# A hybrid decoder layer on one core: the first MLP layer by seven half-size products per pair of units, and the MLP in eight blocks of four tiles

## The reference

```python
x = x + gt1 * mix
h2 = rmsnorm(x, norm2_g) * (1.0 + sc2) + sh2
x = x + gt2 * (jnp.square(jax.nn.relu(h2 @ w_ff1)) @ w_ff2)
...
y = rmsnorm(x, final_g)          # D_MODEL = 1024, D_FF = 4096
```

## Time and profile before

| | us |
|---|---|
| median of 3 runs (lowest, highest) | 1261.55 (1257.51, 1267.34) |
| the profiled execution | 1263.77 |
| its span, first to last instruction | 1262.0 |
| TensorE busy in it | 1195.5 (7549 matmuls) |
| VectorE, ScalarE, GpSimd busy | 439.0, 401.8, 431.5 |

### The profile page before, as it was taken

One profiled execution on the slowest core, in us unless ns is written; L12 is line 12 of the kernel. 1 busy time (PEld: TensorE's weight loads), 2 busy tenths in 40 slices (PEclk: granted clock), 3 DMA queues, 4 the chain that ended last, 5 costly groups with the idle time before them and its releaser, 6 DMA issues.

```text
span 1262.0 us, 19541 instructions
## 1 busy us (share of the span) xinstructions
PE 1195.5 (95%) x7549; PEld 1143.7 (91%) x7549; DVE 439.0 (35%) x812; ACT 401.8 (32%) x675; POOL 431.5 (34%) x322
## 2 busy tenths in 40 slices
PE   4899999789988999999999999999999999999997
PEld 2698888679876899899999999999999999999996
DVE  4651445367785434631111122111121111211125
ACT  4642445335334334543111233111333101332121
POOL 0431111100543348664322344221444212444441
PEclk9999989879987999999999999999999999999998
DMA  9704424535531721111111111111110111111103
GB/s 313 271 32 133 118 79 153 171 109 182 171 106 63 252 101 68 67 35 50 51 50 36 48 50 50 51 33 50 50 50 33 50 50 50 41 43 50 33 1 135
DMA packets 56301, 109.73 MB, mean 87 GB/s; under 512 B 6418, under 2 KB 28854, under 8 KB 55862
## 3 DMA queue, kind: packets, MB, share of 16 engines
q1 hardware_dynamic: 46038, 84.88, 19.9%
q10 hardware_dynamic: 10208, 24.12, 6.1%
HBM read 96.81 MB, written 12.18 MB: 86 GB/s over the span
## 4 chain that ended last, share of the span: by engine, by line
PE 78%; DVE 9%; DMA 6%; ACT 3%; SPq 2%; issue 1%; POOL 0%; ACTq 0%; DVEq 0%; POOLq 0%
PE D L1707 24%; PE D L1709 23%; PE D L1708 23%; DMA RAWW<-in_WADA 2%; PE X L1678 1%; PE X L1734 1%; PE X L1735 1%; PE X L1736 1%; DMA X0T<-in_x 1%; DMA out_C_p<-CN 1%; DMA NM<-nm_d 1%; DVE FU L1271 1%; PE X L1692 1%; DVE X L1285 1%; DVE FU L1475 1%
## 5 line engine op out<-in xcount | busy, mean ns | idle before, releaser
L1707 PE MATMUL D<-H_hi,W_hi 128*128 128x344 f32 x1144 | 376.9, 329 | 2.0 <-POOL H_lo L825 1.3
L1708 PE MATMUL D<-H_lo,W_hi 128*128 128x344 f32 x1144 | 369.4, 323 | 0.0
L1709 PE MATMUL D<-H_hi,W_lo 128*128 128x344 f32 x1144 | 369.0, 323 | 0.0
L820 POOL TENSOR_TENSOR W_lo<-RAWW,W_hi 128x1024 fp32r<-128x1024 f32 x84 | 201.7, 2401 | 410.9 <-ACT W_hi L962 409.7
L1707 PE MATMUL D<-Y_hi,W_hi 128*128 128x344 f32 x936 | 300.9, 321 | 3.1 <-issue 2.9
L1708 PE MATMUL D<-Y_lo,W_hi 128*128 128x344 f32 x936 | 299.6, 320 | 0.0
L1709 PE MATMUL D<-Y_hi,W_lo 128*128 128x344 f32 x936 | 299.6, 320 | 0.0
L1707 PEld LDWEIGHTS D<-H_hi,W_hi 128*128 128x128 f32 x1144 | 219.1, 192 | 12.5 <-issue 8.4
L1708 PEld LDWEIGHTS D<-H_lo,W_hi 128*128 128x128 f32 x1144 | 218.8, 191 | 0.7 <-issue 0.2
L1709 PEld LDWEIGHTS D<-H_hi,W_lo 128*128 128x128 f32 x1144 | 218.5, 191 | 0.0
L825 POOL TENSOR_TENSOR Y_lo<-FU,Y_hi 128x344 f32 (+3 forms) x120 | 113.6, 949 | 230.2 <-ACT Y_hi L967 229.9
(11 more groups left out here) (280 smaller groups left out, 946.0 us busy)
## 6 DMA issues: line engine op xcount, KB each, us to landing
RAWW<-in_W SPq DMA_DIRECT2D x76, 512.0 KB, 3.2
RAWW<-in_WADA ACTq DMA_DIRECT2D x28, 512.0 KB, 4.3
RAWW<-in_WADA SPq DMA_DIRECT2D x20, 512.0 KB, 7.5
RAWW<-in_W ACTq DMA_DIRECT2D x18, 512.0 KB, 3.3
X0T<-in_x SPq DMA_DIRECT2D x3, 1376.0 KB, 9.4
X<-in_x SPq DMA_DIRECT2D x8, 516.0 KB, 6.2
out_y<-OUTN SPq DMA_DIRECT2D x24, 172.0 KB
NM<-nm_d SPq DMA_DIRECT2D x8, 256.0 KB, 4.6
```

The source lines that it names most:

```text
L820: nc.gpsimd.tensor_tensor(lo_v, RAWW[:, raw, :] if src is None else src[:], hi_v.bitcast(F32), ALU.subtract).then_inc(w_lo_ready, 1)
L1707: T.matmul(out, w_h, hi[:, kt, a:b], start=(kt == 0), stop=False)
L1708: T.matmul(out, w_h, lo[:, kt, a:b], start=False, stop=False)
L1709: one = T.matmul(out, w_l, hi[:, kt, a:b], start=False, stop=(kt == KT - 1))
```

## The change

For 14 of the 16 pairs of first-layer units, chunks 1 and 2 are computed by Strassen's method in Winograd's form. Take a pair's weights as A11, A12 (first unit, first and last four tiles of the input) and A21, A22 (second unit), and the input as B11, B21 (chunk 1, first and last four tiles) and B12, B22 (chunk 2). Instead of eight half-size products there are seven: A11 by B11, A12 by B21, S2 by T2, S1 by T1, S3 by T3, A22 by T4, S4 by B22, with S1 = A21+A22, S2 = S1-A11, S3 = A11-A21, S4 = A12-S2 (VectorE, once per pair) and T1 to T4 likewise of the input (once in all; each is split in hi and lo too). The seven land in five PSUM banks X0 to X4; VectorE adds them up (`summed`, `joined`) through three SBUF tiles `KEPT`. Chunk 0 is computed as before (`direct`). The first four units stay as they were.

The MLP becomes `FF_PARTS` = 8 blocks of four hidden tiles: two pairs of the first layer, then 24 second-layer products of four tiles each (12 matmuls) instead of 24 of eight. The weights' hi and lo now lie in a ring of six half-unit places (`place`), which ScalarE (`ring`) and VectorE (`low`) write; GpSimd no longer makes weights' lo parts in the MLP. A load for the second layer has the four tiles of two units (two pieces of 2 KB per partition). `B1` and `B2` hold the second norm's output of chunks 1 and 2, which no longer passes through `FU`. The loop now runs over whole blocks: blocks 0, 1 and 7 are written out, five are one loop. The last block takes units 4 to 7 chunk by chunk, and half of chunk 1's final pieces come after the last inverse.

```diff
--- before.py
+++ after.py
...
 FF_BLOCKS = 4
+FF_T = 4
+FF_PARTS = KT // FF_T * FF_BLOCKS
...
+        HALF_AT = {"A11": 0, "A12": 1, "S2": 2, "S1": 3, "S3": 4, "A21": 5, "A22": 6, "S4": 7}
...
+        SEVEN = {"A11": ("X0", 0), "A12": ("X1", 0), "S2": ("X2", 0), "S1": ("X3", 0), "S3": ("X4", 0), "A22": ("X0", 1), "S4": ("X1", 1)}
...
+        def place(l, n=1):
+            k = (l + 4) % 6
+            assert k % 2 + n <= 2
+            return tuple(t[k // 2][:, (k % 2) * HALF:(k % 2 + n) * HALF] for t in (RING_HI, RING_LO))
...
+        PIECES = [(0, 0), (0, 1), (1, 2), (1, 0), (1, 1), (0, 2)]
...
+        def second_steps(last):
+            out = [(0, k % 2, k // 2) for k in range(2 * NCH)] + [(1, k // NCH, k % NCH) for k in range(2 * NCH)]
+            if last:
+                return out + [(2 + k % 4 // 2, k % 2, k // 4) for k in range(4 * NCH)]
+            return out + [(f, k // NCH, k % NCH) for f in (2, 3) for k in range(2 * NCH)]
...
+            def ring(b, i, name):
+                prev = (b[0], b[1] - 1)
+                if name == "F":
+                    act.wait_ge(raw_in[raw_tile(FF_T + i)], raw_landed(b, FF_T + i))
+                elif name[0] == "A":
+                    t = 2 * i + (name != "A1")
+                    act.wait_ge(raw_in[raw_tile(t)], raw_landed(b, t))
+                else:
+                    act.wait_ge(sums_ready, per_pair(b, i, 4, {"S2": 2, "S1": 2, "S4": 3, "S3": 4}[name]))
+                if name == "F":
+                    if is_first(b):
+                        if i in (0, 2):
+                            act.wait_ge(d_full[NCH - 1], D_FIRST + 2 + i)
+                    elif i == 0:
+                        seven_there(act, b, 1, "S2")
+                        seven_there(act, b, 1, "S1")
+                    elif i == 1:
+                        seven_there(act, b, 1, "S3")
+                        act.wait_ge(d_full[1], direct_at(b, 1))
+                    elif i == 2:
+                        seven_there(act, b, 1, "A22")
+                        seven_there(act, b, 1, "S4")
+                    if i == 3:
+                        act.wait_ge(d_full[NCH - 1], second_at(b, NCH - 1, 2))
+                elif name == "A22":
+                    seven_there(act, b, i, "A11")
+                elif name == "S4":
+                    seven_there(act, b, i, "A12")
+                elif i == 0:
+                    n = {"A1": 4, "S2": 5, "S1": 6, "S3": 7, "A21": 8}[name]
+                    act.wait_ge(d_full[NCH - 1], second_at(prev, NCH - 1, n))
+                elif name == "A1":
+                    seven_there(act, b, 0, "S2")
+                    seven_there(act, b, 0, "S1")
+                elif name == "S2":
+                    seven_there(act, b, 0, "S3")
+                elif name == "S1":
+                    act.wait_ge(d_full[1], direct_at(b, 0))
+                elif name == "S3":
+                    seven_there(act, b, 0, "A22")
+                elif name == "A21":
+                    seven_there(act, b, 0, "S4")
+                nc.scalar.activation(ring_half(i, name)[0], ring_source(i, name), ACT.Copy).then_inc(ring_hi, 1)
...
+            def keep_first(b, i):
+                seven_there(act, b, i, "A11")
+                nc.scalar.activation(KEPT[0][:], seven_bank("A11"), ACT.Copy).then_inc(first_kept, 1)
+            def pair(b, i):
+                ring(b, i, "A21")
+                if i:
+                    hi_piece(b, 0, 5)
+                relu_piece(b, i, 0)
+                hi_piece(b, i, 0)
+                keep_first(b, i)
+                ring(b, i, "A22")
+                ring(b, i, "S4")
+                hi_piece(b, i, 1)
+                if i == 0:
+                    ring(b, 1, "A1")
+                    ring(b, 1, "S2")
+                else:
+                    ring(b, 0, "F")
+                hi_piece(b, i, 2)
+                relu_piece(b, i, 1)
+                if i == 0:
+                    ring(b, 1, "S1")
+                else:
+                    ring(b, 1, "F")
+                hi_piece(b, i, 3)
+                if i == 0:
+                    ring(b, 1, "S3")
+                hi_piece(b, i, 4)
...
+            def t_sum(n):
+                b11, b21, b12, b22 = (t[:, k:k + FF_T, :] for t in (B1, B2) for k in (0, FF_T))
+                if n == 0:
+                    dve.wait_ge(lo_ready, P_FF)
+                    one = V.tensor_tensor(b22, b22, b12, ALU.subtract)
+                elif n == 1:
+                    one = V.tensor_tensor(b12, b12, b11, ALU.subtract)
+                elif n == 2:
+                    one = V.tensor_tensor(b11, b22, b11, ALU.add)
+                else:
+                    one = V.tensor_tensor(b21, b21, b11, ALU.subtract)
+                tell(one, t_summed, n + 1)
+            def low(b, i, name):
+                dve.wait_ge(ring_hi, ring_at(b, i, name))
+                hi_v, lo_v = ring_half(i, name)
+                V.tensor_tensor(lo_v, ring_source(i, name), hi_v.bitcast(F32), ALU.subtract).then_inc(ring_lo, 1)
+                if name[0] == "S":
+                    dve.wait_ge(ring_lo, ring_at(b, i, name))
...
+            def sums_12(b, i):
+                for t in (2 * i, 2 * i + 1):
+                    dve.wait_ge(raw_in[raw_tile(t)], raw_landed(b, t))
+                tell(V.tensor_tensor(SB[:], raw_half(2 * i + 1, 0), raw_half(2 * i + 1, 1), ALU.add), sums_ready, per_pair(b, i, 4, 1))
+                tell(V.tensor_tensor(SA[:], SB[:], raw_half(2 * i, 0), ALU.subtract), sums_ready, per_pair(b, i, 4, 2))
+            def sum_4(b, i):
+                tell(V.tensor_tensor(SA[:], raw_half(2 * i, 1), SA[:], ALU.subtract), sums_ready, per_pair(b, i, 4, 3))
+            def sum_3(b, i):
+                tell(V.tensor_tensor(SB[:], raw_half(2 * i, 0), raw_half(2 * i + 1, 0), ALU.subtract), sums_ready, per_pair(b, i, 4, 4))
+            def slot_of(b, i, q):
+                dve.wait_ge(lo_ready, piece_at(b, i, q) - (FUS - 1))
+                return FU[:, piece_tile(i, q)[3], 0:CH]
...
+            def joined(b, i, q, name, k):
+                fu = slot_of(b, i, q)
+                seven_there(dve, b, i, name)
+                tell(V.tensor_tensor(fu, seven_bank(name), KEPT[k][:], ALU.add), seven_free[SEVEN[name][0]], seven_at(b, i, name))
+                V.scalar_tensor_tensor(out=fu, in0=fu, scalar=0.0, in1=fu, op0=ALU.max, op1=ALU.mult).then_inc(full_ready, 1)
+            def summed(b, i, name, src, dst):
+                seven_there(dve, b, i, name)
+                one = V.tensor_tensor(KEPT[dst][:], seven_bank(name), KEPT[src][:], ALU.add)
+                if name == "S1":
+                    link(one)
+                else:
+                    tell(one, seven_free[SEVEN[name][0]], seven_at(b, i, name))
...
+            def pair(b, i):
+                if i:
+                    joined(b, 0, 5, "S4", 2)
+                low(b, i, "A21")
+                squared(b, i, 0)
+                low(b, i, "A22")
+                dve.wait_ge(first_kept, per_pair(b, i, 1, 1))
+                joined(b, i, 1, "A12", 0)
+                low(b, i, "S4")
+                summed(b, i, "S2", 0, 1)
...
+                    sums_12(b, 1)
+                summed(b, i, "S1", 1, 2)
+                if i == 0:
+                    low(b, 1, "A1")
+                else:
+                    low(b, 0, "F")
+                summed(b, i, "S3", 1, 1)
+                joined(b, i, 2, "S1", 1)
+                if i == 0:
+                    low(b, 1, "S2")
+                    sum_4(b, 1)
+                squared(b, i, 3)
+                if i == 0:
+                    low(b, 1, "S1")
+                    sum_3(b, 1)
+                else:
+                    low(b, 1, "F")
+                joined(b, i, 4, "A22", 1)
+                if i == 0:
+                    low(b, 1, "S3")
+            def residual(b, o, f, h, c):
...
+            def next_part(b, o):
+                after = (b[0], b[1] + 1)
+                if o == 13:
+                    low(after, 0, "A1")
+                elif o == 14:
...
+                for o, (f, h, c) in enumerate(second_steps(False)):
+                    residual(b, o, f, h, c)
+                    if o == 1:
+                        low(b, 2, "F")
+                    elif o == 7:
+                        low(b, 3, "F")
...
-                    final(0, range(6, KT))
+                elif QUAD + 5 <= o <= QUAD + 7:
+                    k = 2 * (o - QUAD - 5)
+                    final(0, range(k, k + 2))
+                elif o == QUAD + 8:
                     inverse_diagonal(1)
...
+                elif o == QUAD + 10:
+                    final(1, (0,))
+                elif o == QUAD + 11:
+                    final(1, range(1, 4))
             inverse_diagonal(NCH - 1)
+            final(1, range(4, KT))
             final(NCH - 1, range(POOL_FIN, KT))
 
 
@@ -1882,13 +2243,69 @@
                     pe.wait_ge(d_free[bank], g * 2 + (first - SKEW + v))
```

(43 more changed lines are left out.)

499 lines of the change are left out of this document (304 added, 195 removed).

## The result

The changed kernel takes 1229.85 us (median of 4 runs, 1229.13 to 1230.67), the kernel before 1261.8 us beside it (4 runs, 1257.51 to 1267.34). The profiled execution took 1229.13 us, its span is 1227.2.

The account below looks back on a forecast made before the run. TensorE was taken as the bound, busy 95% of the span. Terms -26.4 + 2.1 + 0.5 + 0.5 = -23.3 us on 1263.8 gave 1240.5, or 1238.3 from the runs' median, stated as 1239; range 1233 to 1253.

Parts of the forecast that it names:

- the base and the lower end of the range: Whole kernel: profiled 1263.8 us as base, runs' median 2.2 lower; range reaching down to 1233 by the runs' own spread.
- The removed matmuls: MLP on TensorE: 168 fewer matmuls at 0.1574 us each save 26.4 us.
- Rival 4: TensorE in the MLP: starts of groups set the pace, so 330 products for 192 eat the saving; no chance given.
- The opening piece: Each second-layer start: the hidden piece read first comes 0.3 us late, 2.1 us over seven blocks, bounds 0 and 8.4.
- Rival 1: VectorE's strict order delays last pieces around 1.2 us per block start or pair: 8.4 instead of 2.1, about 1245; chance 0.15.
- These edits I cost at nothing: Weight copies and lo parts in the MLP's ring of places: weights arrive in time, cost 0.
- The step into the MLP: Entry to the MLP: VectorE's input sums and lo parts delay piece 9, costing 0.5 us, bounds 0 and 2.
- The tail: Behind the last inverse: four more VectorE pieces and queued stores cost 0.5 us, bounds 0 and 1.5.
- Rival 2: MLP loop: body too long to be kept, four jumps back stall TensorE, 12 to 20 us, 1251 to 1259; chance 0.12.
- Rival 3: Second-layer starts: lateness of about 3.5 us per block drops TensorE's clock, 34 us for seven blocks, 1272; chance 0.06.

Follow-up runs that it names:

- e1: The kernel before, unchanged, run again: 844.4 us from the first output-projection product to the end of the span, instead of 841.5.
- e4: The kernel before with only its small buffers moved to the SBUF places the change gives them: ratio 0.9988 to the kernel before.
- e10: The kernel before, unchanged, once more: output projection starts at 415.23 us.
- e11: The kernel before, unchanged, a second copy: output projection starts at 411.69 us.
- e3: The changed kernel with each pair's A11 product done twice, putting 168 matmuls back: MLP 709.82 us, from 683.38.
- e5: The changed kernel with VectorE's lo part of F1 behind the join of piece 4 in each block's second pair: MLP 1.04 us shorter.
- e7: The changed kernel with two unused VectorE additions between relu and square of the piece opening the second layer: MLP 689.64 us, 6.26 added.
- e6: The changed kernel with VectorE's lo parts of F2 and F3 later, in the first block only: MLP 0.52 us shorter.
- e8: The changed kernel with five unused VectorE additions ahead of the opening piece's square: MLP 29.28 us longer, ratio 1.0013 to the kernel before.

## Why the prediction was off, step by step

**The step that failed: the base and the lower end of the range.** The prediction says that the range "reaches down by the runs' own spread: 1233". I had taken the part ahead of the MLP as a constant, read from one execution, with 2.2 us between it and the median of three runs as its only uncertainty. It isn't one: the start of the output projection stands anywhere between 411.7 and 423.8 us in five profiles of the old form and between 410.2 and 422.5 in nine of the new. The profile that I worked from was a late one (420.45), and the first four runs of the changed kernel were luck: 1229.13 to 1230.67, at the low end of its sixteen, which go to 1244.5. The same kernel in two other sessions took 1233.9 and 1234.3 us, at the lower edge of the range but in it. The 29 runs of the kernel before beside e1 to e4 go from 1253.5 to 1271.7 us, down to 7.6 below their median; that much below 1238.3 would have been 1230.7, at the edge of what was measured. The terms of the change were not the fault: I had them at 23.3 us together, and the stages give 24.56 less 0.6 and 0.3 (below), 23.7. What the sum also lacked is a term for the part ahead of the MLP, which I had at nothing; by the run times of the next paragraph it is about 4 us.

How much of the 32 us is real? The stages give 24.56 - 0.6 = 24 us. The three comparisons of the unchanged pair gave 32, 27 and 31 us less on the whole (1229.85 to 1261.8, 1233.9 to 1261.06, 1234.34 to 1265.24). The mean of all sixteen runs of the changed kernel is 1234.3 us, that of the 92 of the kernel before in the same sessions (e1, e10 and e11 among them) 1262.4: 28.1 us less, to within some 2.6 by the scatter of the runs. e3 says the same: by its stages it should be 2.5 us longer than the kernel before, and its median is 0.3 shorter. The stages agree with both only if the part ahead of the MLP gave something too. Its end, the first landmark, stands at 540.3 us in the mean of the five old forms and at 537.1 in that of the nine new ones, 3.2 us earlier in spite of the longer wait there; 2.1 of it is there at the start of the output projection (417.8 and 415.6), the rest is the late load of e1 and e11. With a spread of 4 us in each group this difference of means alone could be chance. Another reading of the profiles goes the same way: in the first 40 us the nine new forms made 134 to 146 matmuls, mean 142, the five old ones 126 to 136, mean 133; at 100 us the distance is still 10, at 6.6 matmuls per us 1.5 us. The places of the small buffers are not its cause (e4 has 126). What is, and whether the distance holds in more copies, stays open. So 24 us are shown to come from the change, some 4 more are likely by the run times but not explained, and the rest of the first pair's 32 is chance. Why the clock falls there in one execution and not in the next stays open as well.

**The removed matmuls, -26.4.** Right: 26.44 in e3. Rival 4 (group starts eat the saving) is out by the same number and by the block's period, 86.83 us in e5.

**The opening piece, +2.1 (0.3 x 7; bounds 0 to 8.4).** Right in mechanism, half in size: 1.04 us by e5, 0.16 in each turn of the loop and some 0.1 in the blocks before and behind it. The chain went as forecast up to VectorE's hold, but Y_lo, started 0.81 us before the lo part's end, finished 0.78 behind it where I had 0.95. That difference of 0.17 is about what the forecast of 0.3 was too high. Rival 1 (1.2 us per block) asked for another 1 us of lateness in VectorE's list; no row of the changed kernel shows it. e7, where the piece is 1.0 us later, shows what it would have cost: 6.3 us more, as much as the 8.4 - 2.1 = 6.3 that I had between it and the forecast.

The row which the prediction lacked, GpSimd as the loser, is there now: 1.59 us instead of 0.93 when VectorE holds, and VectorE 3.89 instead of 1.22 when GpSimd does. The Trainium skill, page "SBUF — State Buffer", section "Who interferes with whom", says that the first to issue blocks the other fully. The trace agrees with the order in both directions. The whole instruction is not held back, though: Y_lo would then have ended at 641.24 + 0.93 = 642.17, and it ended at 642.02. VectorE's lo part beside T_lo likewise ended 1.08 us behind T_lo and not 1.22. So some 0.15 us of the second one runs beside the first, whichever it is.

**The cost that I put at nothing and was not: the weights of the first block, +0.5.** "These edits I cost at nothing" covered the lo parts of F2 and F3 beside GpSimd's lo parts of T. I had seen that overlap for the squares in the step into the MLP, and had GpSimd's T_lo in the same paragraph, but did not put the two lists side by side for VectorE's new work. By e6 it is 0.52 us.

**The step into the MLP, +0.5.** Measured 0.6 (1.00 against 0.39 us of wait, and the same in all nine new-form profiles). **The tail, +0.5.** From the last square to the end of the span there are 11.2 to 12.7 us in the five old-form profiles and 11.7 to 12.9 in the nine new ones, mean 11.8 and 12.1: 0.3, within the scatter. All stall terms together: 3.1 forecast, 1.9 in the MLP and 0.6 to 0.9 outside it measured. With every term right, the sum would still have been 1263.8 - 26.4 + 2.6 = 1240.0 on the profiled execution.

**Rival 2, the loop body.** Out: no idle time without a releaser in the MLP, turns of the loop as long as the written-out block once the opening stall is gone (86.83 us, e5), and 42 instruction packets instead of 34 for the whole run.

**Rival 3, the clock.** It didn't happen, but e8 shows that its mechanism and its point were right: with a stall of 3.25 us per block nothing is left of the gain, where the prediction had "about 3.5 us per block". Only its price per dip was high, 1.6 us and in five of seven cases, where I had 2 in each.

## What to carry to other kernels

Before summing up terms of a few tenths of a microsecond, measure how far the unchanged part repeats: one profile gives the size of a stage but not where it stands, and the range of a forecast on the whole is at least that of the old kernel's own runs. Measure an edit by the time between two landmarks that enclose only what it touches; here it repeats to 0.01 us while the total moves by 10. A part that the edit doesn't touch needs as many copies as it takes to tell its two means apart; five and nine were too few here. When work moves to another engine, lay the new list of that engine beside the lists of those with which it can't run together, in every stage, the first block too.

## What the hardware showed that I had not expected

- The same program reached the same instruction at 411.7 to 420.5 us (four copies of the old kernel) and at 410.2 to 422.5 (three of the new). By 40 us from the start, while DMA is above 90% busy, profiles are already 12 matmuls apart (80 and 92 in the window from 20 to 40 us of the first pair).
- A stall of 3.25 us behind some 80 us of even work brought TensorE to 1.2 GHz five times out of seven, for some 12 matmuls, 1.6 us of loss (e8). The 2.9 us in front of the output projection were followed by 9 to 12 such matmuls in all fourteen profiles, the waits of 2.47 and 2.07 us in e1 and e11 by 12 and 11. Stalls of 1 us or less in the same stages never were.
- VectorE and GpSimd hold each other in both directions: whichever starts second ends late, GpSimd 1.59 us instead of 0.93, VectorE 3.89 instead of 1.22, each some 0.15 us earlier than if it had begun at the other's end.
- A loop body of 552 matmuls with their weight loads runs without a gap at its jump back: 86.83 us in e5, as the same block written out.
